# Gate and expert stage of a retrieval block in one block of instructions, coefficients two tiles behind, and one softmax

## The chip, the cores and the metric

The kernel runs on one core of a Trainium2 chip. The time is that of the device in microseconds (us), from the first to the last instruction of the core. The median of three runs is given; beside it stands one execution taken by the hardware profiler, from which every row comes. Five engines work side by side, each on its own list of instructions, and wait for one another by semaphores: TensorE (PE in the rows, its weight loads PEld), VectorE (DVE), ScalarE (ACT), GpSimd (POOL) and SyncE (SP). An engine's name with a q behind it is its instruction queue, where it issues transfers. Sixteen DMA engines move the data.

## What is computed

A decoder block on 512 tokens of width 1024: two token mixers in parallel (a short gated convolution and a gated delta rule), and then a retrieval of experts. The change lies in the retrieval, cut here to its core:

```python
q = (h @ w_q).reshape(B, T, HEADS, 2, 128)           # 8 heads, 2 halves
s = einsum('bthpd,hpnd->bthpn', q, sub_keys)          # 128 keys per half
v1, i1 = top_k(s[..., 0, :], 16); v2, i2 = top_k(s[..., 1, :], 16)
top_s, pos = top_k(v1[..., :, None] + v2[..., None, :], 16)
eidx = take(i1 * 128 + i2, pos)                       # 16 of 16384 experts per head
gates = softmax(top_s)
act = gelu(einsum('btd,bted->bte', h, u_tab[eidx]))
out = einsum('bte,bted->btd', gates * act, v_tab[eidx])
x = x + gt2 * rmsnorm(out, norm_post_ffn)
```

## The kernel before

The 512 tokens are four tiles of 128. Three of them (384 tokens) are computed densely: the products with all 16384 rows of u_tab are made in 128 tiles of 128 experts ("U tiles"), GELU is applied, the result is multiplied with a dense matrix of gates that is zero almost everywhere (the coefficient), and the product with the rows of v_tab ("V tiles") is summed in six PSUM banks. The fourth tile (the "fetched" or own tokens) is treated sparsely: GpSimd fetches one expert row per token at a time (line 201), 128 rows of u_tab and 128 of v_tab, and VectorE multiplies and sums them. Four row buffers are used in turn, so a fetch waits until the row four before it is used.

All products are made in three parts, with every operand split in a high and a low part: ScalarE makes the high part of a weight tile (1024 elements in each partition), GpSimd or VectorE the low part, and a U tile is 24 matmuls, a V tile 18. Three stages follow one another, each an `nc.Block()`, at whose end all engines meet at a barrier.

**Retrieval** (retrieve_stage). TensorE makes the 16 query pieces, then 68 U tiles (`early`). For the fetched tokens the top-k of eight heads runs first on VectorE (`topk(VA, ...)`), then `shift(VO, ...)`, the list of rows `own_row` (line 1653) and a softmax of their own (lines 1631 to 1654). ScalarE makes its Exp at line 1511, in the order of its list between U piece 0 and U piece 1. Then follows the top-k of the dense tokens with `shift(VP, ...)` and `softmax(VP, ...)` at its end. GpSimd makes the low parts (line 1527); from the sixth U piece on its list has a fetch ahead of each of them.

**Gates** (scatter_stage). The dense gates are made by one-hot matrices: six rounds of eight units of 8 tokens. VectorE makes hot1 (line 1739) and the weighted hot2 (line 1744); for units 3 and 7 ScalarE makes hot2 (lines 1815 and 1821). TensorE multiplies them (line 1787), ScalarE copies the result to `gate_block` (line 1834), SP stores it in four quarters of 512 KB (line 1861). Beside this run six U tiles a round (line 1795), behind units 0, 1, 2, 4, 5 and 6. In the last round the last two of them stand behind unit 7. SP also issues the first two U tiles (line 1867) and four V tiles (line 1869) of the next stage, and at the end waits for all its stores (line 1895). The GELUs of the 104 U tiles made before the expert stage are stored in DRAM.

**Experts** (expert_stage). 24 of the U tiles remain, and all 128 V tiles. TensorE alternates: U tile p+1, then V tile p, and for the last 104 V tiles there is no U tile beside. For each tile p ScalarE makes GELU, the high parts of U tile p+2, of the coefficient (`split_c`) and of V tile p+1; VectorE the low part of U tile p+1, of V tile p, the coefficient (line 2117), its low part and one to three fetched rows (`own_rows_at`). SP loads U tiles, V tiles, the stored GELUs and, once for four tiles, the gates (lines 1948 and 1963). At the end the four token tiles are normalized and stored one by one.

## Time and profile before

| | us |
|---|---|
| median of 3 runs | 1856.44 (1854.17 to 1859.69) |
| span of the profiled execution | 1856.8 |
| TensorE busy | 1768.2 (95%) |
| VectorE busy | 1307.3 (70%) |
| GpSimd busy | 764.5 (41%) |
| ScalarE busy | 742.8 (40%) |
| matmuls of the V tiles, three groups | 294.6, 294.5, 294.1 |
| mean granted clock of TensorE | 0.981 |

The share of an engine is an average over stages that have different limits. TensorE's matmuls are pipelined: a duration of one reaches into the next, so starts are to be compared and not durations summed. The granted clock is given as a share of full speed (1.0 is 2.4 GHz, 0.5 is 1.2 GHz).

### The profile page before, as it was taken

How to read it: one execution, taken by the hardware profiler on the slowest of the kernel's cores; microseconds unless marked ns; L12 is line 12 of the kernel's file. 1: busy time of each engine (PE TensorE's matmuls, PEld its weight loads, DVE VectorE, ACT ScalarE, POOL GpSimd, SP SyncE). 2: the span in 40 equal slices, each digit the busy share in tenths (PEclk: the TensorE clock that was granted, in tenths of full speed). 3: DMA queues.
4: the chain of work that ended last, by engine and by line, in shares of the span. 5: the costliest groups of instructions: out<-in, count | busy, mean ns of one | idle time of the engine just before them, and what ended most of it. 6: DMA issues, size and time to landing. Idle time of an engine off the chain costs nothing. (4 is left out here: it accounts for less than half of the span.)

```text
span 1856.8 us, 31058 instructions
## 1 busy us (share of the span) xinstructions
PE 1768.2 (95%) x11485; PEld 1564.7 (84%) x11485; DVE 1307.3 (70%) x2777; ACT 742.8 (40%) x1227; POOL 764.5 (41%) x449
## 2 busy tenths in 40 slices
PE   3999999999998989999999999879999999999998
PEld 2666888878877889999999999879998888888887
DVE  5993454553224679878869999756787888777777
ACT  4332332242234233333337767633333333333334
POOL 2333232344442448777753333122454443332330
PEclk9998999999999999999999999989999999999999
DMA  9661101022322249888868999978899999889883
GB/s 356 217 233 71 36 16 34 25 91 91 102 79 103 91 141 314 282 292 292 286 235 281 341 311 331 319 264 285 287 317 337 370 370 359 326 320 328 316 325 145
DMA packets 179267, 432.64 MB, mean 233 GB/s; under 512 B 15816, under 2 KB 91720, under 8 KB 179040
## 3 DMA queue, kind: packets, MB, share of 16 engines
q1 hardware_dynamic: 125088, 273.71, 42.5%
q0 software_dynamic: 36864, 134.23, 20.3%
q10 hardware_dynamic: 17216, 23.36, 3.4%
q8 instruction: 63, 1.03, 0.2%
q14 instruction: 36, 0.29, 0.0%
HBM read 383.54 MB, written 47.71 MB: 232 GB/s over the span
## 5 line engine op out<-in xcount | busy, mean ns | idle before, releaser
L201 POOL DMA_INDIRECT own_rows<-in_peer_v_dram,own_row x128 | 212.3, 1659 | 330.8 <-DVE y_own L2094 312.7
L1988 PE MATMUL banks<-v_hi,coef_lo 128*128 128x512 f32 x756 | 294.6, 390 | 0.0
L1988 PE MATMUL banks<-v_lo,coef_hi 128*128 128x512 f32 x756 | 294.5, 390 | 0.0
L1988 PE MATMUL banks<-v_hi,coef_hi 128*128 128x512 f32 x756 | 294.1, 389 | 0.1
L201 POOL DMA_INDIRECT own_rows<-in_u_rows_dram,own_row x128 | 160.6, 1255 | 233.1 <-DVE own_rows L1733 178.8
L2079 DVE TENSOR_TENSOR v_lo<-weight_ring,v_hi 128x1024 fp32r<-128x1024 f32 x128 | 156.5, 1222 | 24.7 <-ACT v_hi L2027 22.7
L1988 PEld LDWEIGHTS banks<-v_hi,coef_hi 128*128 128x128 f32 x756 | 142.0, 188 | 29.5 <-issue 0.5
L1988 PEld LDWEIGHTS banks<-v_hi,coef_lo 128*128 128x128 f32 x756 | 141.9, 188 | 29.5
L1988 PEld LDWEIGHTS banks<-v_lo,coef_hi 128*128 128x128 f32 x756 | 141.9, 188 | 28.9
L2094 DVE SCALAR_TENSOR_TENSOR y_own<-own_rows,own_coef,y_own 128x1024 f32<-128x1024 f32 x128 | 163.8, 1279 | 1.9 <-DVE y_own L2094 0.5
L1397 PE MATMUL banks<-h_hi,wring_hi 128*128 128x384 f32 (+2 forms) x448 | 155.2, 347 | 4.0 <-ACT gelu_early L1479 2.9
L2027 ACT ACTIVATE v_hi<-weight_ring 128x1024 fp32r<-128x1024 f32 x128 | 135.1, 1055 | 59.4 <-PE banks L1988 48.1
L1527 POOL TENSOR_TENSOR wring_lo<-weight_ring,wring_hi 128x1024 fp32r<-128x1024 f32 x54 | 129.6, 2399 | 65.4 <-ACT wring_hi L1469 65.3
L1397 PE MATMUL banks<-h_lo,wring_hi 128*128 128x384 f32 (+2 forms) x448 | 154.0, 344 | 0.0
L1397 PE MATMUL banks<-h_hi,wring_lo 128*128 128x384 f32 (+2 forms) x448 | 153.9, 344 | 0.0
L2031 ACT ACTIVATE coef_hi<-coef 128x384 fp32r<-128x384 f32 x128 | 67.0, 524 | 211.6 <-DVE coef L2117 211.6
L1469 ACT ACTIVATE wring_hi<-weight_ring 128x1024 fp32r<-128x1024 f32 x54 | 57.3, 1061 | 158.4 <-PE banks L1397 157.9
L1665 DVE SCALAR_TENSOR_TENSOR own_rows<-own_rows,banks 128x1024 f32<-128x1024 f32 x64 | 77.8, 1215 | 52.3 <-DMA own_rows<-in_u_rows_dram,own_row 52.3
L2079 DVE TENSOR_TENSOR coef_lo<-coef,coef_hi 128x384 fp32r<-128x384 f32 x128 | 71.3, 557 | 57.5 <-ACT coef_hi L2031 57.5
L2117 DVE TENSOR_TENSOR coef<-gelu,gate_tiles 128x384 f32<-128x384 f32 x128 | 70.8, 553 | 45.8 <-ACT gelu L2041 45.8
L1165 POOL TENSOR_TENSOR wring_lo<-weight_ring,wring_hi 128x1024 fp32r<-128x1024 f32 x26 | 64.1, 2465 | 88.7 <-ACT wring_hi L1185 88.7
L1787 PE MATMUL banks<-query_hot 128*128 128x128 f32 x768 | 93.6, 278 | 6.7 <-ACT gate_block L1834 5.0
(393 smaller groups left out, 4346.1 us busy)
## 6 DMA issues: line engine op xcount, KB each, us to landing
weight_ring<-in_peer_v_dram SPq DMA_DIRECT2D x128, 512.0 KB, 5.4
weight_ring<-in_peer_u_dram SPq DMA_DIRECT2D x68, 512.0 KB, 4.5
ada<-in_w_ada_dram SPq DMA_DIRECT2D x48, 512.0 KB, 5.7
gate_scratch<-gate_block SPq DMA_DIRECT2D x48, 512.0 KB, 7.0
gate_tiles<-gate_scratch SPq DMA_DIRECT2D x32, 768.0 KB, 6.9
gelu_scratch<-gelu_early ACTq DMA_DIRECT2D x104, 192.0 KB
gelu<-gelu_scratch SPq DMA_DIRECT2D x104, 192.0 KB, 5.6
u_early<-in_peer_u_dram SPq DMA_DIRECT2D x36, 512.0 KB, 7.1
```

The lines of the kernel that those rows point to most:

```text
L201: pool.indirect_dma_start(own_rows[:, n % R], None, tables[n // NS], bass.IndirectOffsetOnAxis(ap=own_row[:, n % NS:n % NS + 1], axis=0)). ...
L1165: nc.gpsimd.tensor_tensor(w_lo[:, b % 2], wring[:, b], w_hi[:, b % 2].bitcast(F32), ALU.subtract).then_inc(lo_ready, 1)
L1397: last = nc.tensor.matmul(out, ww[n % HR][:, k, :], x[:, k, t0:nt], start=(k == 0 and m == 0), stop=(k == KT - 1 and m == 2))
L1527: nc.gpsimd.tensor_tensor(w_lo[n % HR][:], w[:, n % WR], w_hi[n % HR][:].bitcast(F32), ALU.subtract).then_inc(lo_ready, 1)
L1665: nc.vector.scalar_tensor_tensor(rows[:, i % R], rows[:, i % R], 1.0, h_psum[:], ALU.mult, ALU.mult, accum_out=own_act[:, bass.ds(n, 1)]). ...
L1787: last = nc.tensor.matmul(bank[2 * (u % 2) + t // 4][:, t % 4 * P:(t % 4 + 1) * P], hot1[:, u % RH, t, :], hot2[:, u % RH, t, :], start=Tr ...
L1988: last = nc.tensor.matmul(y_bank(t, half)[:], w[:, j, t * P:(t + 1) * P], x[:, j, c], start=(first and n == 0), stop=False)
L2027: nc.scalar.activation(v_hi[:, e % G], vt[:, e % G], ACT.Copy).then_inc(v_hi_ready, 1)
L2031: nc.scalar.activation(c_hi[:, e % G], coef[:, e % 2], ACT.Copy).then_inc(c_hi_ready, 1)
L2079: return nc.vector.tensor_tensor(dst, src, hi.bitcast(F32), ALU.subtract)
L2094: nc.vector.scalar_tensor_tensor(y_own[:], rows[:, n % R], own_coef[:, n - NS:n - NS + 1], y_own[:], ALU.mult, ALU.add).then_inc(row_used, 1)
L2117: nc.vector.tensor_tensor(by_block(coef[:, p % 2]), by_block(gel[:, j]), gt[:, i % 2, :, j, :], ALU.mult).then_inc(coef_ready, 1)
```

## The change

Three edits. First, the barrier between gates and experts goes: both stages are written into one `nc.Block()`, the semaphores of both are made ahead of it (`scatter_sems`), and TensorE waits for the copy of unit 6 instead. SP issues U tiles 2 and 3 of the expert stage behind the last stores and only then waits for the stores; the wait for the stored GELUs moves from ScalarE to SP. In the last round the U tiles stand where they do in the other rounds, and unit 7 gets its hot2 from VectorE. Tiles in SBUF are laid out in another order, and `y_own` is zeroed behind the wait for the first gate tile. Second, LAG = 2: in the expert stage the coefficient and everything behind it are made two tiles later; TensorE runs U tile m and then V tile m-3. Third, in the retrieval the softmax of the fetched tokens is no longer made ahead of the dense top-k; one softmax over all four token tiles is made at the end.

```diff
                 retrieve_stage(nc, a, env, acts)
-                scatter_stage(nc, a, env, spill, acts)
-            expert_stage(nc, a, env, spill, acts, out)
+                scatter_sems(env)
+                block = late.enter_context(nc.Block())
+                scatter_stage(nc, a, env, spill, acts, block)
+            expert_stage(nc, a, env, spill, acts, out, block)
...
                     if m == 0:
                         copy(0)
-                        act.wait_ge(*VO.after("gsub"))
-                        nc.scalar.activation(gates[:, ND], gates[:, ND], ACT.Exp).then_inc(own_exp, 1)
...
                 act.wait_ge(*VP.after("gsub"))
-                nc.scalar.activation(gates[:, 0:ND], gates[:, 0:ND], ACT.Exp).then_inc(exped, 1)
+                nc.scalar.activation(gates[:], gates[:], ACT.Exp).then_inc(exped, 1)
...
                 dve.wait_ge(*VA.after("sel1", PH - 1))
-                shift(VO, ND, TT)
...
-                softmax(VO, ND, TT, own_gate[:].rearrange("p (h k) -> p h k", h=PH), "own_gate")
...
-                shift(VP, 0, ND)
-                softmax(VP, 0, ND, th(gates[:, 0:ND]), "gates")
+                total, top = (gsum[:, n].rearrange("p t h -> p (t h)") for n in range(2))
+                nc.vector.tensor_copy(top, th(score)[:, :, 0]).then_inc(*VP.step("gmax"))
+                dve.wait_ge(*VP.after("gmax"))
+                nc.vector.tensor_tensor(th(gates), th(score), top.unsqueeze(2).to_broadcast([P, TT * PH, TOPK]), ALU.subtract).then_inc(*VP.step("gsub"))
...
+                nc.vector.tensor_tensor(own_gate[:].rearrange("p (h k) -> p h k", h=PH), gates[:, ND], top[:, ND * PH:TT * PH].unsqueeze(2).to_broadcast([P, PH, TOPK]),
+                                        ALU.mult).then_inc(*VP.step("own_gate"))
...
-        tiles = {False: {u: (m,) for m, u in enumerate(U_UNITS)},
-                 True: {**{u: (m,) for m, u in enumerate(U_UNITS[:-2])}, NU - 1: (U_ITER - 2, U_ITER - 1)}}
+        tiles = {u: (m,) for m, u in enumerate(U_UNITS)}
...
+        def act_makes(u, final):
+            return u in by_act and not (final and u == NU - 1)
...
+            body(NR - 1, True)
+            pe.wait_ge(*A.after(f"unit{NU - 2}", NR - 1))
...
+            for q in range(1, NQ):
+                store(NR * SLOTS - 1, 1, q)
+            for m in range(2, 4):
+                sp.wait_ge(u_lo_ready, m - 1)
+                sp.dma_start(ut[:, m % 2], a["peer_u"][N_EARLY + m]).then_inc(s_u[m % 2], 16)
+            for s in stored:
+                sp.wait_ge(s, 16 * NQ * (NR + 1))
+            for s in s_gel:
+                sp.wait_ge(s, G0 + 16 * (NR * U_ITER // 2))
...
+        LAG = 2
...
+            for j in range(G):
+                u_products(j, j % 2)
+                if j > LAG:
+                    y_products(j - LAG - 1, j - LAG - 1, first=(j == LAG + 1))
+            with pe.Fori(1, GL) as i:
+                for j in range(G):
+                    u_products(i * G + j, j % 2)
+                    y_products(i * G + (j - LAG - 1), (j - LAG - 1) % G)
+            with pe.Fori(GL, GX) as i:
+                for j in range(G):
+                    y_products(i * G + (j - LAG - 1), (j - LAG - 1) % G)
...
+            for m in range(NX + LAG):
+                p = m - LAG
...
+                if m < NL:
+                    act.wait_ge(u_done, m + 1)
+                    nc.scalar.activation(gel[:, m % G, :], bank[m % 2][:, 0:TD], ACT.Gelu).then_inc(gelu_ready, 1)
+                if m + 2 < NL:
+                    split_u(m + 2)
+                if p >= 0:
                     split_c(p)
                     if p + 1 < NX:
                         split_v(p + 1)
...
+            n = U_DONE
+            for m in range(NX + LAG):
+                p = m - LAG
+                if m + 1 < NL:
+                    split_u(m + 1)
+                if p < 0:
+                    continue
...
+                if p == 0:
+                    nc.vector.memset(y_own[:], 0.0).then_inc(own_zero, 1)
```

## Rows read from the trace of the kernel before

**Rows 1.** Windows: us, busy us (instructions) of each engine, PEclk, DMA share, GB/s

```profile
683.30:689.40 6.10, 6.09 (x19) 6.09 (x20) 1.97 (x14) 1.43 (x2) 4.53 (x5) 0.50 0.79 253
1202.00:1206.00 4.00, 4.00 (x21) 4.00 (x21) 0.00 (x0) 1.08 (x2) 0.00 (x0) 0.65 0.07 20
1206.80:1215.00 8.20, 6.34 (x37) 6.02 (x35) 3.99 (x6) 2.04 (x3) 1.35 (x1) 1.00 0.95 292
1225.00:1228.00 3.00, 3.00 (x10) 3.00 (x11) 1.94 (x2) 1.94 (x2) 0.00 (x0) 0.50 0.70 171
1500.00:1600.00 100.00, 100.00 (x443) 82.84 (x442) 82.28 (x99) 37.89 (x51) 38.57 (x23) 1.00 0.96 357
```

**Rows 2.** Waits of TensorE from 560 us on: us in total, times, longest

```profile
PE banks L1978 <- PEq L1726: 11.8, 1, 11.8
PE banks L1787 <- ACT gate_block L1834: 5.0, 1, 5.0
PE banks L1397 <- POOL wring_lo L1527: 0.7, 1, 0.7
```

**Rows 3.** The chain that ended last, from 1224.95 us: start, us, work

```profile
1224.95 10.31 PE banks L1978 x48
...
1239.39 4.18 PE banks L1978 x24
...
1426.29 416.44 PE banks L1988 x1836
```

**Rows 4.** Timeline of TensorE at the gates' end: start, us, instruction, wait before

```profile
1192.16 3.73 PE L1787 MATMUL banks<-query_hot 128*128 128x128 f32 x32
1200.88 3.78 PE L1787 MATMUL banks<-query_hot 128*128 128x128 f32 x16 [4.98 <-ACT gate_block L1834]
```

**Rows 5.** Timeline of ScalarE in the same stretch

```profile
1194.20 2.45 ACT L1815 ACTIVATE query_hot<-cst,idxT 128x128 f32<-128x128 f32 x8 [0.40 <-PE banks L1787]
...
1199.77 2.01 ACT L1834 ACTIVATE gate_block<-banks 128x512 f32<-128x512 f32 x4
1204.70 1.08 ACT L1834 ACTIVATE gate_block<-banks 128x512 f32<-128x512 f32 x2 [2.91 <-PE banks L1787]
```

**Rows 6.** Timeline of VectorE in the same stretch

```profile
1188.81 2.15 DVE L1744 TENSOR_SCALAR query_hot<-cst,idxT,gateT 128x128 f32<-128x128 f32 x8
1190.86 1.23 DVE L1739 TENSOR_TENSOR query_hot<-cst,idxT 128x1024 f32<-128x1024 f32 x1
...
1211.01 1.23 DVE L1758 TENSOR_TENSOR wring_lo<-u_tile,wring_hi 128x1024 fp32r<-128x1024 f32 x1 [16.33 <-ACT wring_hi L1847]
```

**Rows 7.** Line 1867, U tiles 0 and 1, issued at 1176.5 and 1180.7

```profile
DMA to landing us min/median/max: 9.6/10.8/12.0
```

**Rows 8.** Timeline of all engines at the start of the U pieces

```profile
680.20 0.31 ACT L1511 ACTIVATE gates<-gates 128x128 f32<-128x128 f32 x1 [3.99 <-DVE gates L1646]
...
680.40 0.23 DVE L1653 CAST own_row<-own_row_f 128x128 uint32<-128x128 f32 x1
...
683.31 0.69 PE L1397 MATMUL banks<-h_hi,wring_hi 128*128 128x384 f32 x1 [2.94 <-ACT gelu_early L1479]
...
684.04 1.14 POOL L201 DMA_INDIRECT own_rows<-in_u_rows_dram,own_row  x1 [0.16 <-issue]
...
690.38 1.22 DVE L1665 SCALAR_TENSOR_TENSOR own_rows<-own_rows,banks 128x1024 f32<-128x1024 f32 x1 [4.97 <-DMA own_rows<-in_u_rows_dram,own_row]
...
692.85 2.40 POOL L1527 TENSOR_TENSOR wring_lo<-weight_ring,wring_hi 128x1024 fp32r<-128x1024 f32 x1
```

**Rows 9.** Timeline of VectorE among the V tiles

```profile
1434.44 1.22 DVE L2079 TENSOR_TENSOR v_lo<-weight_ring,v_hi 128x1024 fp32r<-128x1024 f32 x1
1435.58 0.55 DVE L2117 TENSOR_TENSOR coef<-gelu,gate_tiles 128x384 f32<-128x384 f32 x1
1436.05 1.28 DVE L2094 SCALAR_TENSOR_TENSOR y_own<-own_rows,own_coef,y_own 128x1024 f32<-128x1024 f32 x1
1437.24 0.55 DVE L2079 TENSOR_TENSOR coef_lo<-coef,coef_hi 128x384 fp32r<-128x384 f32 x1
```

## What I expect of the change, and why

> **What bounds the kernel now.** I read the windows first, then the waits of TensorE, then the chain of waits, and last the timelines of single engines around each wait. In the expert stage TensorE is busy 100.00 of 100 us at a granted clock of 1.00, and the DMA engines are near their limit beside it (share 0.96, 357 GB/s) [rows 1]. The chain of waits says the same: from 1426.29 us one piece of 1836 matmuls runs for 416.44 us, which is 102 tiles of 4.08 us, and a product with a U tile takes 4.18 us for 24 matmuls [rows 3]. So from 1224.95 us to the end nothing but matmuls counts, and a gain has to come from places where TensorE stands still. From the retrieval on the change touches four: 11.8 us at the block boundary (PEq L1726), 5.0 us for a copy of the gates (gate_block), 2.9 us for a GELU at the start of the retrieval, 0.7 us for a wring_lo behind it [rows 2, 8]. Each idle stretch of 2.9 us or more also drags a slow one behind it: after the 2.94 us the granted clock was 0.50 for 6.1 us, which is 1.2 of 2.4 GHz, and at the start of the expert stage again 0.50 [rows 1]. There 48 matmuls took 10.31 us [rows 3], where two U tiles at full clock take 2 x 4.18 = 8.36: 1.95 us lost. After the 5 us wait 16 matmuls took 3.78 us where 32 took 3.73 before it [rows 4]: 1.9 us again.
>
> **The boundary between gates and experts.** Reference point: TensorE finishes unit 4 and U tile 3 of the last round, then units 5 and 6 start at 1192.16, and U tile 1 of the expert stage ends at 1224.95 + 10.31 = 1235.26 [rows 3, 4]. In between lie 3 units (3.73 / 2 = 1.87 with the pipeline's end, 1.75 from start to start) and 4 U tiles of 4.18: 5.25 + 16.7 = 22.0 us of work in 43.1 us. So 21.1 us are lost here, of which 16.8 are the two waits and about 4 are clock.
>
> The change moves three things. (1) Unit 7 of the last round gets its weighted one-hot from VectorE instead of ScalarE. On ScalarE it is the eight L1815 from 1194.20 and the L1821 up to the next copy at 1199.77, 5.6 us in front of the copies of units 5 and 6 [rows 5]; that is what TensorE waited 5.0 us for. On VectorE it costs 8 selections in 2.15 us behind the 1.23 us comparison that it makes already [rows 6]; VectorE stood idle for 16.33 us up to 1211.01, so this is hidden. Before that idle time it split tile 5, ready at 1194.7, and that can't come earlier; unit 7 is then ready at 1194.7 + 3.3 = 1198.0. (2) The last two U tiles go behind units 5 and 6. TensorE then runs unit 5 from 1192.16, tile 4, unit 6, tile 5, unit 7 without a wait and ends at 1192.16 + 5.25 + 8.36 = 1205.8; unit 7 is asked for at 1204.0, long after 1198.0. (3) The barrier goes; U tile 0 of the expert stage follows at once (its split is done by 1202) and ends at 1209.95.
>
> What is late next is on ScalarE and on SP's queue. ScalarE copies unit 7 at 1205.9 to 1207.0 (1.08 us [rows 5]), makes a v_hi and the hi part of U tile 1 (about 1.05 each), VectorE the lo part: 1210.3, a wait of 0.4 us, so TensorE ends U tile 1 at 1214.5. U tile 2 is the trouble. SP issues it behind the four stores of the last gate block, and these wait for the copy of unit 7, now 1207.0 where it was 1205.8. Before, the engines were busy with these stores from 1206.8 to 1215.0 at a share of 0.95 and 292 GB/s, two GELU stores included [rows 1]. Shifted, the stores hold the engines from 1208.0 to 1216; U tile 2 (512 KB, 1.5 us at the 357 GB/s of [rows 1]) is queued behind them, and up to three fetched rows that now fall in the same time take their share. I take a landing at 1218.5; hi, lo and hand-over take 2.5 us, so U tile 2 starts at 1221.0. The bounds: 1219.0 if the rows are all through before the stores, and 1224.9 if it lands 12.0 us after an issue at 1210.4, as the slower of the two first U tiles did in a full queue [rows 7]; I stay near the lower end because the engines were all but empty from 1202 to 1206 (share 0.07 [rows 1]), where now the first rows go. Then TensorE was idle 6.5 us and restarts at the lower clock; I charge 1.95 us as before. Gain of the boundary: 1235.26 - 1221.0 - 1.95 = **12.3 us** (8.4 to 14.3).
>
> The Trainium skill, page "DMA: Bandwidth & Descriptors", section "Queues, rings and completion order", says that on each engine the descriptors of one queue are consumed in ring order. By that rule U tile 2 can't pass the stores, which is the case that I take; the 9.6 to 12.0 us of the two loads issued into a busy queue [rows 7] agree with it.
>
> What SP issues behind: the first gate tile now waits for the last store (about 1216.5) and is queued behind U tiles 2 and 3. It would land near 1224, at worst 12 us after its issue, 1228.5. The coefficient of tile 0 is two tiles later than before: V tile 0 is multiplied only after U tile 3, at about 1231. VectorE stands at this load with the lo part of U tile 4 queued behind it, needed at 1235. Both are met; cost nothing, and if the load came after 1229.5 each us would count. U tile 4 is behind two gate tiles of 768 KB; it lands near 1226 and is needed after 1227. The zeroing of y_own (0.9 us) moves behind the gate wait on VectorE, in the same cover.
>
> **From U tiles to V tiles alone.** The coefficient of tile p is now finished by ScalarE after the GELU of tile p+2. While U and V products alternate (8.3 us a pair) this leaves slack on both sides. When the U tiles end, ScalarE makes coef_hi of tile 21 only after the GELU of tile 23, and tiles 21, 22 and 23 have three fetched rows each on VectorE. One such tile costs 1.14 (v_lo) + 0.47 (coef) + 0.47 (coef_lo) + 3 x 1.19 = 5.65 us, from start to start [rows 9], against 4.08 us of TensorE. With the end of U tile 23 as zero, coef_lo of 21 is ready at 1.5, of 22 at 7.1, of 23 at 12.8 and of 24 at 18.0; TensorE asks for them at 4.1, 8.2, 12.3 and 17.0. That is 0.6 + 1.0 = **1.6 us lost** (0 if VectorE is further ahead, 4 if a row lands late).
>
> **The retrieval's softmax.** Before, ScalarE stopped at the Exp of the fetched tokens (started 680.20) and split the next weight piece only afterwards; VectorE had its list of rows at 680.40, and GpSimd could fetch only at 684.04 behind the split that came late; TensorE stood from 680.37 to 683.31 [rows 8]. Removed are one Exp with its two table loads on ScalarE and five small VectorE operations. Now ScalarE splits at 676.2, when U piece 1 ends, GpSimd needs 2.4 us [rows 8], and the fetch starts with the list, at 680.4: 3.6 us earlier. But the next GpSimd split (692.85) stands behind a fetch that waits for the first row used, and the row takes 6.3 us (684.04 to 690.38) [rows 8]. So this split ends at 691.6 instead of 695.25. TensorE has its work up to 680.37 + 2 x 4.18 = 688.7 and waits 2.9 us there, in place of 2.94 us before the slow stretch and 0.7 after it. The next start is 3.6 us earlier. Whether the clock falls again costs 0 to 3.1 us (6.1 us at half clock were the 3.1); I take 1.7, since the wait is about as long as the one that did it. Gain **1.9 us** (0.5 to 3.6), and TensorE is the bound for the rest of the retrieval, so it lasts. At the end the joint softmax is 512 instead of 384 elements wide for shift, Exp and sum, and one product is added: about 0.5 us on VectorE, most of it beside U tiles and transposes. I charge 0.1 us (0 to 0.5).
>
> **Sum.** -12.3 - 1.9 + 0.1 + 1.6 = -12.5 us on the profiled 1856.8 us, 1844.3. The median of the runs is 0.4 us lower, so **1844.0 us**.
>
> **Rivals.** (a) The load lands late: rows and stores share the engines and U tile 2 lands up to 12 us after its issue. Then it starts at 1224.9, the boundary gives 8.4 and the whole 8.6: 1847.8. For it speaks the store rate of 292 GB/s at a share of 0.95, against it that only 1.5 MB of rows are in the way. (b) U tile 2 is not held by the stores and lands while U tile 1 runs. Then there is neither wait nor slow clock: the boundary gives 1235.3 - 1214.5 = 20.8 and the time is 1835.4. It needs the load to overtake 2 MB that were issued before it. (c) The backlog of fetched rows at the end of the U tiles is not worked off at once, because rows are fetched one by one behind VectorE: 6 instead of 1.6 us, 1848.4. (d) The stall is moved and not removed: the stage of V tiles alone starts with empty buffers and gives back what the boundary gained, 1853 to 1856. Against it, the time per tile there was that of TensorE. (e) Slower: DMA becomes the bound of the V tiles alone. There 35.7 MB move in 100 us, 24.5 tiles, 1.46 MB a tile; at 357 GB/s this is 4.08 us, exactly TensorE's tile. If loads and rows bunch differently, so that only 340 GB/s come through, a tile takes 4.28 us, and 104 tiles cost 21 us: 1865. It decides from 4.20 us a tile, 347 GB/s; the share of 0.96 leaves little room, but what is moved and when it is asked for stays the same.
>
> **Chances.** Forecast (U tile 2 starts by 1223, 1841 to 1846.5) 0.55; (a) 0.19; (b) 0.08; (c) 0.08; (d) 0.06; (e) 0.04. The likeliest case gives 1844.0. The range reaches from the early end of the boundary (1842 less 3.6 for the retrieval and the U end without loss) to beyond (a) and (c): 1838.5 to 1850.0. A measurement of this kernel tells about 0.3%, 5.6 us, from no change. Faster: 0.55 + 0.19 + 0.08 + 0.08, less 0.02 for (a) and (c) together, 0.88; same: (d) and that 0.02, 0.08; slower: (e), 0.04.
>
> **What would show it.** Right: no 5.0 us and no 11.8 us wait of TensorE; unit 7 followed at once by a product of the expert stage; then one wait of 5 to 8 us before U tile 2, released by the lo part of that tile, with its load landing 8 to 9 us after its issue; in the retrieval a wait of about 3 us before the sixth U piece, released by GpSimd, and none for the GELU; two short waits of about 1 us each when the U tiles end, released by coef_lo; V tiles of 4.08 us. Wrong: a wait for gate_tiles on VectorE that reaches TensorE, a V tile above 4.1 us over a long stretch, or the first U tile of the expert stage waiting for its split.

## The result, and the profile of the changed kernel

| | before | changed kernel |
|---|---|---|
| median of 20 runs, us | 1858.59 | 1860.37 |
| lowest to highest, us | 1854.17 to 1864.41 | 1857.77 to 1866.41 |
| profiled span, us | 1856.8 | 1857.5 |

The ratio is 1.0016 with a 95% interval of 1.0008 to 1.0023. The forecast was 12.5 us less; the median rose by 1.8 us, far below the 2% from which a change counts as one. The waits that were to go are gone all the same. These are TensorE's waits from 560 us on in the changed kernel (line waited at, what ended the wait: us in total, times, longest), to be laid beside [rows 2]:

```profile
PE banks L1990 <- DVE wring_lo L2093: 8.9, 2, 8.8
...
PE banks L1399 <- POOL wring_lo L1527: 2.3, 1, 2.3
PE banks L2000 <- DVE coef_lo L2093: 2.0, 2, 1.1
```

The 11.8 us and the 5.0 us have gone. One wait of 8.8 us before U tile 2 has come, and two of about 1 us for coef_lo at the end of the U tiles. Now the chain of waits from the last gate unit on (start, us, work), which answers to [rows 3]:

```profile
1198.80 1.80 PE banks L1793 x16
...
1200.62 1.09 ACT gate_block L1841 x2
...
1202.79 5.59 SPq L1866
...
1208.42 1.45 SPq L1866
...
1209.91 5.82 DMA u_tile<-in_peer_u_dram
...
1218.13 9.91 PE banks L1990 x48
1228.04 4.20 PE banks L2000 x18
1232.24 4.18 PE banks L1990 x24
...
1414.71 428.64 PE banks L2000 x1836
```

Two readings. TensorE began U tile 2 at 1218.13 us and two U tiles were done at 1228.04, where before it was 1235.26: TensorE is 7.2 us ahead there, with two U tiles of 4.18 us more behind it, 15.6 us in all. And in the last line 1836 matmuls take 428.64 us where they took 416.44 [rows 3]. They begin 11.6 us earlier (1414.71 against 1426.29) and last 12.2 us longer. That is the whole difference of the two profiles. Three windows of the changed kernel (us, busy us and instructions of each engine, granted clock, DMA share, GB/s) say what it isn't:

```profile
682.00:686.00 4.00, 4.00 (x25) 4.00 (x24) 2.19 (x10) 1.44 (x2) 1.88 (x2) 1.00 0.91 316
...
1214.00:1218.00 4.00, 0.00 (x0) 0.00 (x0) 1.15 (x1) 2.24 (x3) 0.00 (x0) 0.52 1.00 361
...
1500.00:1600.00 100.00, 100.00 (x430) 80.60 (x429) 78.72 (x94) 37.20 (x49) 38.10 (x21) 1.00 0.88 332
```

In the first, behind the old place of the 2.9 us wait, TensorE works at full clock, where it had 0.50 before [rows 1]. In the second it stands and waits for U tile 2 while the DMA engines are busy throughout. In the last one TensorE is busy for all 100 us at a granted clock of 1.00, as in [rows 1], but gets through 430 matmuls instead of 443. It waits for nothing, the clock is full, and the DMA engines have become less busy (0.88 for 0.96): each matmul takes longer. The timeline of TensorE shows the step (start, us, instruction):

```profile
1499.72 0.39 PE L2000 MATMUL banks<-v_lo,coef_hi 128*128 128x512 f32 x1
1499.95 0.40 PE L2000 MATMUL banks<-v_hi,coef_lo 128*128 128x512 f32 x1
1500.18 0.39 PE L2000 MATMUL banks<-v_hi,coef_hi 128*128 128x512 f32 x1
1500.42 0.40 PE L2000 MATMUL banks<-v_lo,coef_hi 128*128 128x512 f32 x1
1500.65 0.39 PE L2000 MATMUL banks<-v_hi,coef_lo 128*128 128x512 f32 x1
1500.88 0.40 PE L2000 MATMUL banks<-v_hi,coef_hi 128*128 128x512 f32 x1
```

From start to start it is (1500.88 - 1499.72) / 5 = 232 ns; over the whole stretch 428.64 / 1836 = 233.5 ns, before 416.44 / 1836 = 226.8. In these 102 tiles the 6.7 ns a matmul make 12.2 us. A V tile that stands between two U tiles takes 4.20 us in the chain above, and before it was this:

```profile
1243.57 4.12 PE banks L1988 x18
```

That is 0.08 us a tile or 1.9 us for the 24 of them, so that the slower V matmuls cost about 14 us altogether. The U tiles kept their 4.18 us.

The change does one thing that the section on it names in half a sentence, that its diff leaves out and that the prediction gave no price. It lays out the SBUF tiles of the expert stage in another order:

```diff
-        gel = sb(ctx, "gelu", [P, G, TD])
...
         v_hi = sb(ctx, "v_hi", [P, G, D], F32R)
         v_lo = sb(ctx, "v_lo", [P, G, D], F32R)
-        gt = sb(ctx, "gate_tiles", [P, 2, TD // TB, G, TB])
+        own_coef = sb(ctx, "own_coef", [P, NS])
+        ss = sb(ctx, "y_sq", [P, 4, TT])
         coef = sb(ctx, "coef", [P, 2, TD])
+        gel = sb(ctx, "gelu", [P, G, TD])
         c_hi = sb(ctx, "coef_hi", [P, G, TD], F32R)
         c_lo = sb(ctx, "coef_lo", [P, G, TD], F32R)
-        own_coef = sb(ctx, "own_coef", [P, NS])
...
+        gt = sb(ctx, "gate_tiles", [P, 2, TD // TB, G, TB])
...
-        ss = sb(ctx, "y_sq", [P, 4, TT])
```

Tiles are put one behind another, and y_sq has 64 bytes a partition (4 x 4 fp32). Before it was the last of them. Now it stands ahead of coef_hi and coef_lo, and moves them by 64 bytes against v_hi and v_lo: coef_hi begins at byte 191008 of a partition before and at 179296 now, v_hi at 142880 and 136736. Modulo 256 these are 32 for both before, and 96 against 32 now. Every other tile that lies or lay between the two is a multiple of 256 bytes long, and so is the distance from v_hi to v_lo and from coef_hi to coef_lo.

### The profile page after: what moved, and what is told of

It is laid out like the page before. It is cut to its first block and busy times, and to the rows that moved or that the text cites. A ratio compares the mean times of both kernels' runs of the same rounds, so it can differ in the third digit from the quotient of the medians.

```text
span 1857.5 us, 31015 instructions
## 1 busy us (share of the span) xinstructions
PE 1775.6 (96%) x11485; PEld 1558.8 (84%) x11485; DVE 1311.6 (71%) x2781; ACT 736.1 (40%) x1208; POOL 768.6 (41%) x449
## 5 line engine op out<-in xcount | busy, mean ns | idle before, releaser
L201 POOL DMA_INDIRECT own_rows<-in_peer_v_dram,own_row x128 | 217.1, 1696 | 332.9 <-DVE y_own L2108 315.5
L2000 PE MATMUL banks<-v_hi,coef_hi 128*128 128x512 f32 x756 | 298.9, 395 | 2.0 <-DVE coef_lo L2093 2.0
L2000 PE MATMUL banks<-v_hi,coef_lo 128*128 128x512 f32 x756 | 298.8, 395 | 0.0
L2000 PE MATMUL banks<-v_lo,coef_hi 128*128 128x512 f32 x756 | 298.8, 395 | 0.0
L1801 PE MATMUL banks<-h_hi,wring_hi 128*128 128x384 f32 x288 | 99.2, 345 | 0.0
L1527 POOL TENSOR_TENSOR piece_lo<-weight_ring,piece_hi 128x1024 fp32r<-128x1024 f32 x28 | 67.1, 2397 | 72.4 <-ACT piece_hi L1471 72.3
```

The source lines that it names most:

```text
L201: pool.indirect_dma_start(own_rows[:, n % R], None, tables[n // NS], bass.IndirectOffsetOnAxis(ap=own_row[:, n % NS:n % NS + 1], axis=0)). ...
L1527: nc.gpsimd.tensor_tensor(w_lo[n % HR][:], w[:, n % WR], w_hi[n % HR][:].bitcast(F32), ALU.subtract).then_inc(lo_ready, 1)
L1801: last = nc.tensor.matmul(bank[4 + m % 2][:, 0:TD], ww[:, m % 2, k, :], x[:, k, 0:TD], start=(k == 0 and n == 0), stop=(k == KT - 1 and n ...
L2000: last = nc.tensor.matmul(y_bank(t, half)[:], w[:, j, t * P:(t + 1) * P], x[:, j, c], start=(first and n == 0), stop=False)
```

## The experiments

In all of them the time is set beside runs of the kernel before on the same chip.

**Is it the layout? (e1, e2).** e1 is the changed kernel with y_sq allocated last again, and nothing else; e2 is the kernel before with 64 bytes put ahead of coef.

```diff
e1:
-        ss = sb(ctx, "y_sq", [P, 4, TT])
         coef = sb(ctx, "coef", [P, 2, TD])
...
         y = sb(ctx, "y", [P, TT, D])
+        ss = sb(ctx, "y_sq", [P, 4, TT])
e2:
+        sb(ctx, "pad", [P, 16])
         coef = sb(ctx, "coef", [P, 2, TD])
```

> The changed kernel with one edit: y_sq, 64 bytes in each partition, is laid out behind y as before the change and no longer between own_coef and coef, so coef, gelu, coef_hi and coef_lo start 64 bytes lower, at 32 modulo 128 as in the kernel before. Theory P (the place of coef_hi and coef_lo in SBUF sets the pitch of the V matmuls): the pitch falls from 233.3 back to 226.7 ns, a V tile from 4.20 to 4.08 us, 128 tiles give 15 us, about 1845 us beside 1858.6 of the kernel before. Rival C (the pitch comes from the new instruction order of TensorE, its loops or the lag of two tiles): pitch and time stay, 233.3 ns and 1860 us. Rival D (from the load on SBUF by the DMA queues and VectorE, which the new order shifts): likewise unchanged.

> The kernel before with one edit: an unused tile of 64 bytes in each partition ahead of coef, so coef, coef_hi and coef_lo start 64 bytes higher, at 96 modulo 128. Theory P: the pitch of the V matmuls rises from 226.7 to 233.3 ns, 128 tiles cost 15 us, about 1874 us. Rivals C and D: 226.7 ns and 1858.6 us, since order and load are those of before.

e1 took 1848.37 us, 0.9950 (0.9932 to 0.9968) of before; e2 took 1871.85 us, 1.0086 (1.0060 to 1.0112). The chain of e1, then that of e2 (whose piece holds 1872 matmuls):

```profile
1415.46 416.40 PE banks L2000 x1836
```

```profile
1417.15 436.90 PE banks L1989 x1872
```

The first is 226.8 ns a matmul, the second 233.4. The same 64 bytes make a fast kernel slow and a slow one fast, with all instructions the same. The theory that the layout is the cause holds, and the queues, the lag and the merged block have no part in the slow matmuls.

**Which placement is good? (e3, e4).** e3 is e1 with 96 bytes behind eps, so that all large tiles begin at a multiple of 128 bytes; e4 is e1 with y_sq between coef_hi and coef_lo, so that only coef_lo is moved.

```diff
e3:
         eps = sb(top, "eps", [P, 1])
+        sb(top, "pad", [P, 24])
e4:
         c_hi = sb(ctx, "coef_hi", [P, G, TD], F32R)
+        ss = sb(ctx, "y_sq", [P, 4, TT])
         c_lo = sb(ctx, "coef_lo", [P, G, TD], F32R)
```

> As the kernel with y_sq last, and 96 unused bytes behind eps, so nearly all large tiles start at 0 modulo 128 instead of 32. If the cost under theory P is one of 128-byte lines that an operand crosses, the fixed 13.3 ns that a 512-column matmul takes beyond 512 columns at 2.4 GHz shrinks in all stages: 7 ns for some 10000 matmuls would be 60 us or more, about 1780 us. If only the step from 32 to 96 matters, pitches stay at 226.7 and 173.3 ns and the time at about 1845 us.

> The changed kernel with y_sq between coef_hi and coef_lo: coef_hi starts at 32 and coef_lo at 96 modulo 128. Theory P with a cost for each matmul whose stationary operand lies at 96: one in three V matmuls uses coef_lo, so the mean pitch is 226.7 + 6.7 / 3 = 228.9 ns, a V tile 4.12 us, and the time about 1850 us. If the cost hangs on coef_hi alone, 226.7 ns and 1845 us; if on any of coef or gelu, which VectorE and ScalarE use, 226.7 ns too.

e3 took 1847.07 us (416.41 us for the 1836): aligning everything gives no more than e1 had. e4 took 1855.74 us, and the groups of instructions by shape show it between 1410 and 1830 us (busy us, mean ns of one; in e1 all three stand at 389):

```profile
L2000 PE MATMUL banks<-v_hi,coef_lo 128*128 128x512 f32 x605 | 240.3, 397 | 0.0
L2000 PE MATMUL banks<-v_lo,coef_hi 128*128 128x512 f32 x605 | 237.2, 392 | 0.0
L2000 PE MATMUL banks<-v_hi,coef_hi 128*128 128x512 f32 x605 | 235.4, 389 | 0.9 <-DVE coef_lo L2093 0.9
```

By these durations the matmul with the moved operand is longer, that before it a little, the third not. A duration reaches into the next matmul, though. From start to start (547 or 548 of each kind between 1440 and 1820 us) the matmul with coef_lo takes 235.9 ns, v_lo with coef_hi 229.2 and v_hi with coef_hi 228.3, where all three take 226.4 to 227.0 in e1. So the one whose operands lie apart loses 9 ns and its two neighbours about 2 each. The 1836 took 424.55 us, 231.2 ns each: two thirds of the loss, where only one matmul in three uses coef_lo. The forecast of a third was wrong, and why the neighbours lose too stays open.

**One operand's place, or the two against each other? (e5, e6, e9, e10).** Each is e1 with pads: 64 bytes ahead of v_hi, behind v_lo and behind coef_lo (e5); 32 bytes ahead of coef_hi (e6); 64 bytes ahead of v_hi alone, which moves v and the coefficients together (e9); 64 bytes ahead of gate_tiles, which leaves all four operands in place (e10). In one diff, with the experiment behind each line (the pads' names differ from file to file):

```diff
+        sb(ctx, "pad_a", [P, 16])   # e5, e9
         v_hi = sb(ctx, "v_hi", [P, G, D], F32R)
         v_lo = sb(ctx, "v_lo", [P, G, D], F32R)
+        sb(ctx, "pad_b", [P, 16])   # e5; [P, 32] in e13, [P, 64] in e14
         own_coef = sb(ctx, "own_coef", [P, NS])
...
+        sb(ctx, "pad", [P, 8])      # e6
         c_hi = sb(ctx, "coef_hi", [P, G, TD], F32R)
         c_lo = sb(ctx, "coef_lo", [P, G, TD], F32R)
+        sb(ctx, "pad_c", [P, 16])   # e5, e10
         gt = sb(ctx, "gate_tiles", [P, 2, TD // TB, G, TB])
```

> The kernel with the sums laid last (1848.4 us), plus three pads of 64 bytes: v_hi and v_lo now begin at 96 of 128 bytes, the coefficients stay at 32, and gate_tiles, y_own and y are at 96 as they are in the changed kernel. Theory 'it is the place of the stationary operand': the V products keep 226.7 ns a matmul (1836 matmuls in 416.4 us) and the time stays within 3 us of 1848.4. Rival 'any fp32 tile of the V products, or the tiles that VectorE and the DMA use beside them, counts': 233.3 ns, 428.5 us, about 1861.

> The kernel with the sums laid last, with a pad of 32 bytes ahead of coef_hi, so that coef_hi and coef_lo begin at 64 of 128 bytes. So far 0 and 32 gave 226.7 ns and 96 gave 233.3. Theory A, a row of 32 bytes more at 96 straddles something that 0 to 64 don't: 226.7 ns, about 1848. Theory B, the half above 64 is the slow one: 233.3 ns, about 1861.

> The kernel with the sums laid last, with one pad of 64 bytes ahead of v_hi: v_hi, v_lo, coef_hi and coef_lo all begin at 96 of 128 bytes, the gate tiles, y_own and y too. So far the V products took 226.7 ns a matmul with both operands at 32 or both at 0, and 233.3 with the operands at different remainders (32 and 96, 96 and 32, 32 and 64). Theory D, only the difference of the two operands' places counts: 226.7 ns, 416.4 us for the 1836, about 1848.4. Theory A, an operand that begins at 64 or above of 128 bytes costs, whichever it is: 233.3 ns, about 1861.

> The kernel with the sums laid last, with one pad of 64 bytes ahead of gate_tiles: all four operands of the V products stay at 32 of 128 bytes, gate_tiles, y_own, y and the sums go to 96. In every slow kernel so far these had moved too. Theories D and A (the operands count): 226.7 ns, about 1848.4. Rival G, it is what VectorE, ScalarE and the DMAs touch beside the matmuls: 233.3 ns, about 1861.

| kernel | v_hi, coef_hi, modulo 256 | difference | 1836 matmuls, us | median, us |
|---|---|---|---|---|
| e1 | 32, 32 | 0 | 416.40 | 1848.37 |
| e3 | 128, 128 | 0 | 416.41 | 1847.07 |
| e9 | 96, 96 | 0 | 416.41 | 1847.19 |
| e10 | 32, 32 | 0 | 416.41 | 1849.40 |
| e14 | 32, 32 | 0 | 416.45 | 1846.57 |
| e6 | 32, 64 | 32 | 428.64 | 1860.81 |
| changed | 32, 96 | 64 | 428.64 | 1860.37 |
| e5 | 96, 160 | 64 | 428.64 | 1859.28 |
| e13 | 32, 160 | 128 | 426.88 | 1858.26 |

Here are the pieces of 1836 matmuls of e6 and then of e9:

```profile
1413.90 428.64 PE banks L2001 x1836
```

```profile
1416.54 416.41 PE banks L2001 x1836
```

My first theory blamed the place of the stationary operand (the coefficients; v is the moving one), and it is e9 that refutes it: with coef_hi and coef_lo at 96 the matmuls are fast if v is at 96 as well, and in the changed kernel, with v at 32, they are slow. e5 does not do so by itself. I counted modulo 128 when I wrote down what I expected of it, and modulo 256 its pads moved the coefficients too, from 32 to 160. e6 came out at the 233 ns of its theory B, that the half above 64 is the slow one, and e9 refutes this as well. e10 clears gate_tiles, y_own, y and y_sq; own_coef, coef and gelu, the other tiles of this stage that the pads shift, are in their old place in the slow e6 and moved in the fast e9. What is left is the difference between the two operands of a product.

**Modulo what? (e13, e14).** e1 with 128 and with 256 bytes ahead of own_coef.

> The kernel with the sums laid last, with a pad of 128 bytes ahead of own_coef: the coefficients begin 128 bytes off the places of v_hi and v_lo, modulo 512. Theory, the difference counts modulo 128 (or a smaller power of two above 32): 226.7 ns, 1848.4 us. Rival, it counts modulo 256 or 512: 233.3 ns, about 1861 us.

> The same with a pad of 256 bytes. Modulo 128 or 256: 226.7 ns, 1848.4 us. Modulo 512: 233.3 ns, about 1861 us.

Their pieces, e13 first:

```profile
1415.59 426.88 PE banks L2001 x1836
```

```profile
1410.17 416.45 PE banks L2001 x1836
```

128 bytes apart is slow (1858.26 us, a shade less: 232.5 ns), 256 apart is fast (1846.57 us). So it counts modulo 256; of the two answers I had thought the other likelier. e13's coefficients were at 128-byte alignment with v_hi, so aligning to 128 bytes would not have been enough. In all slow kernels the coefficients lie 32, 64 or 128 bytes further on than v; other differences were not run.

**Does it hold for other products? (e11).** e1 with 64 bytes between h_hi, h_lo and the weight rings. All that follows moves along, so v and the coefficients still agree, both at 96.

```diff
+        sb(top, "pad", [P, 16])
         ring = sb(top, "weight_ring", [P, WRING, D])
```

> The kernel with the sums laid last, with one pad of 64 bytes between h_hi/h_lo (which stay at 32 of 128 bytes) and the weight rings: the split weights and all that follows go to 96, so that the U products have their operands 64 apart and the V products theirs at the same remainder. Theory D: V products at 226.7 ns (416.4 us for 1836), U products slower, 180.0 instead of 173.3 ns for 384 columns if the same 6.67 ns are added; 24 x 128 of these alone cost 20.5 us and the projections more: 1870 to 1890. Theory A: V products at 233.3 (both at 96), U products slow too: 1883 to 1903. If neither slows: 1848.

It took 1866.34 us, 18.0 more than e1. The V products stayed fast (416.43 us), the U products, with 384 columns, became slower; these are pieces of its chain of waits:

```profile
1405.13 4.24 PE banks L1991 x24
1409.37 4.08 PE banks L2001 x18
1413.45 4.25 PE banks L1991 x24
1437.00 416.43 PE banks L2001 x1836
```

In the retrieval and the gates, over some 2200 matmuls of 384 columns, it is 176.6 ns from start to start for the 173.4 of e1. The direction is as expected, the size is about half of it (3.2 ns where 6.67 were added), and the time lies below the 1870 to 1890 us that were forecast: with 384 columns the loss is smaller than with 512. In the expert stage it hardly shows, since the U tile takes 4.24 for 4.18 us and the V tile beside it 4.08 for 4.12. Most of it comes earlier. The products of 512 columns with the same weights ahead of the retrieval take 233.2 ns for 227 to 228, and the first U piece starts at 677.51 us instead of 664.85.

**The retrieval's term (e7).** e1 with the old, separate softmax of the fetched tokens: the retrieval's hunks of the diff ahead are undone, nothing else.

> The kernel with the sums laid last, but with the softmax of the fetched tokens done by itself at the list of rows, as in the kernel before; everything behind the retrieval is the changed kernel's. My reading of the traces is that the merged softmax gives 4.4 us in the retrieval (forecast: 1.9): so 1848.4 + 4.4 = 1852.8 us, with a wait of 2.9 us for a GELU, a granted clock of 0.50 behind it, and the gate stage starting about 4.4 us later. Rival: the gain belongs to a drift that the projection stage has anyway; then 1849.5 or less.

Its profile has the wait of 2.9 us for the GELU back, the granted clock from 680 to 700 us is 0.83 (0.91 in e1), and the span is 1850.5 us against 1846.0. But its five times are 1852.31, 1848.00, 1852.68, 1848.48 and 1849.03. The median, 1849.03, is 0.7 above e1's and within the rival's "1849.5 or less", and the ratio to before is 0.9950 as in e1: with five runs and four the times don't tell the two apart.

The profiles say more. Of the 4.5 us between the two spans, 1.7 were there before the retrieval's first U piece (666.50 against 664.85 us), where both kernels run the same code. So I measure from the start of this piece to the first matmul of the gates. With the softmax apart this takes 303.5 to 303.7 us (before, e2, e7). With one softmax there are two groups: 299.0 to 299.4 us in the six kernels whose granted clock from 680 to 700 us is 1.00 (the changed kernel, e4, e12, e14, e15, e17), and 300.9 to 302.0 in the nine where it is 0.91 (e1, e3, e5, e6, e8, e9, e10, e13, e16). The edit is worth about 4.4 us if the clock stays up behind the remaining wait for GpSimd, and about 2.3 if it falls.

**The load behind the stores (e8, e12, e15).** In e8 SP issues U tile 2 ahead of the copy of unit 7 and of the last four stores, U tile 3 behind the first.

```diff
e8:
+                    if not more and u == NU - 1:
+                        expert_u(2)
...
+            expert_u(3)
             for q in range(1, NQ):
                 store(NR * SLOTS - 1, 1, q)
-            for m in range(2, 4):
-                sp.wait_ge(u_lo_ready, m - 1)
-                sp.dma_start(ut[:, m % 2], a["peer_u"][N_EARLY + m]).then_inc(s_u[m % 2], 16)
```

> The kernel with the sums laid last, but SP issues U tile 2 of the expert stage ahead of the copy of unit 7 and of the last four stores, and U tile 3 behind the first of these stores. Theory, the 8.5 us wait of TensorE is the load standing behind the issue of the stores: the wait falls below 1 us, no slow clock behind it, and the U tile starts 8 us earlier; the gate tiles still come behind the stores, so a wait of up to 3 us for the first coefficient may take its place. 1848.4 - 8 - 1.5 to - 6: 1839 to 1842.5 us. Rival, the time is given back further on (gate tiles land late, TensorE waits 8 us before V tile 0): 1847 to 1849.

1845.35 us, 3.0 less than e1, where 6 to 9 had been expected. The ratio to before, 0.9942 (0.9924 to 0.9960), is not to be told from e1's 0.9950 (0.9932 to 0.9968). TensorE's waits from 1180 us on before and behind this edit, e1 and then e8:

```profile
PE banks L1990 <- DVE wring_lo L2093: 8.6, 2, 8.5
PE banks L2000 <- DVE coef_lo L2093: 2.6, 2, 1.6
```

```profile
PE banks L2004 <- DVE coef_lo L2097: 10.1, 3, 7.4
...
PE banks L1994 <- DVE wring_lo L2097: 0.2, 1, 0.2
```

The wait for the U tile has gone and one of 7.4 us for the first coefficient has come. VectorE's timeline names its cause, the gate tile, which SP could issue only at 1214.91 us, when the last store had landed:

```profile
1219.30 0.91 DVE L2134 MEMSET y_own<- 128x1024 f32 x1 [5.67 <-DMA gate_tiles<-gate_scratch]
```

e12 therefore stores first the quarter of the last block that holds the first expert tiles, loads the gate tile behind it, and stores the other three quarters after that. The second gate tile and the zeroing of y_own, now one tile later, wait for these.

```diff
e12, SP:
-                        store(i * SLOTS + 1, 1, 0)
+                        store(i * SLOTS + 1, 1, 0 if more else NQ - 1, None if more else g_["last_store"])
...
-            for q in range(1, NQ):
-                store(NR * SLOTS - 1, 1, q)
-            for s in stored:
-                sp.wait_ge(s, 16 * NQ * (NR + 1))
+            sp.wait_ge(g_["last_store"], 16)
...
             sp.dma_start(gt[:, 0], spill[:, tile_at(0) // G]).then_inc(s_g[0], 16)
+            g_["blocks_left"]()
...
                 if j == G - 1 and i < GX - 1:
+                    if not i:
+                        sp.wait_ge(*g_["blocks_out"])
```

> The kernel e8 (U tiles 2 and 3 issued ahead of the last stores), and of the last gate block the quarter that holds the first expert tiles is stored first, with a semaphore of its own; the first gate tile is loaded behind it and the other three quarters are stored after that; y_own is zeroed one tile later. In e8 TensorE waited 7.4 us for the first coef_lo because the gate tile was issued at 1214.9 us and landed at 1219.3. Theory: it is now issued at about 1207 and lands by 1213, the wait for coef_lo falls below 1 us, and the time is 1845.4 - 7 = 1838 us (1836.5 to 1840). Rival, the next load (V or U tile behind the three stores) takes the wait over: 1843 to 1846.

It was slower, 1850.64 us (ten runs, 1846.78 to 1857.10), 5.3 more than e8 and above both what was expected and the rival. The profile is that of the fastest of the ten. The gate tile was used at 1213.26 us, but SP then stood at the wait for the last stores ahead of the second gate tile, with U tile 4 queued behind it:

```profile
1208.77 4.54 SPq L1866 DMA_DIRECT2D gate_scratch<-gate_block  x3
1218.76 0.35 SPq L1983 DMA_DIRECT2D gate_tiles<-gate_scratch  x1
1219.15 0.63 SPq L1971 DMA_DIRECT2D u_tile<-in_peer_u_dram  x1
```

ScalarE waited for that tile 11.94 us and had the coefficient queued behind it; TensorE waited 10.5. e15 puts the last two stores behind U tile 4 and the second gate tile behind U tile 5, and y_own is zeroed at tile 5.

```diff
e15, SP:
+                if p == 4:
+                    g_["blocks_left"](1)
+                    g_["blocks_left"](2)
+                if p == 5:
+                    sp.wait_ge(*g_["blocks_out"])
+                    sp.dma_start(gt[:, 1], spill[:, tile_at(G) // G]).then_inc(s_g[1], 16)
```

> The kernel e12, with the last two stored quarters issued behind U tile 4 and the second gate tile behind U tile 5, so that no load that is due soon stands behind a wait of SP. In e12 the gate tile had landed at 1213.3 us, but ScalarE stood at the hi part of U tile 4, issued at 1219.2, with the coefficient queued behind it, 10.5 us of TensorE. Theory: U tile 4 is issued at 1212 and lands by 1219; the wait for coef_lo falls to 0 to 1 us: 1850.6 - 10 - 2 for the clock: 1836 to 1841 us. Rival, loads, stores and rows share the engines, and whatever is issued first only moves the wait to the next: 1845 or more.

1838.71 us, 0.9897 (0.9880 to 0.9913) of before, in the middle of what was expected, and clear of e1 and e8. The wait at this place is 2.3 us.

**The lag (e16, e17).** e16 is e1, and e17 is e15, with one line changed:

```diff
-        LAG = 2
+        LAG = 1
```

> The kernel with the sums laid last, coefficients one tile behind instead of two. V tile 0 is then due behind U tile 2 and the gate tile is not there yet (VectorE had it at 1221 in the kernel after), and V products wait for the GELU chain within a pair of tiles. Theory: the wait for U tile 2 stays near 8.5, V tile 0 is due at about 1222.5 and waits 2 to 4 us, and the 2.6 us at the end of the U tiles changes to between 0 and 4: 1849 to 1853 us. Rival, the gate tile comes in time because TensorE is late anyway: 1847 to 1848.5.

> The kernel e15 with a lag of one tile. In e15 the first coef_lo came at 1219.1 us although the gate tile had landed at about 1213, because ScalarE makes coef_hi of tile 0 behind the hi part of U tile 4. With the lag of one it stands behind U tile 3, which lands about 1210. Theory: no wait of more than 1 us for coef_lo at the start, and that at the U tiles' end falls from 2.6 us to 0.6 as in e16: 1838.7 - 2.3 - 2.0 = 1834.5 us (1832 to 1837). Rival, V tile 0, due a tile earlier, waits for the gate tile instead: 1837 to 1840.

e16 took 1843.36 us, 5.0 less than e1, where I had expected it to be slower. TensorE's waits from 1180 us on:

```profile
PE banks L1990 <- DVE wring_lo L2093: 9.0, 2, 8.8
PE banks L2000 <- DVE coef_lo L2093: 0.6, 1, 0.6
```

The 2.6 us at the end of the U tiles have become 0.6. V tile 0 did not wait for the gate tile at all: by the chain it follows U tile 2 at once, at 1223.56 us. The other 3 us no wait accounts for. The two kernels ran on different chips, and the runs of the kernel before beside e16 have a median 1.9 us lower (1857.04 against 1858.91); the ratios to before, 0.9928 (0.9911 to 0.9944) and 0.9950 (0.9932 to 0.9968), overlap. In the profiles e16 is 2.9 us ahead when the retrieval's first U piece starts (661.94 against 664.85), where the code is the same. So only the 2.0 us are shown. e17 took 1837.73 us, 0.9891 (0.9871 to 0.9910) of before, the lowest median of all and 22.6 us under the changed kernel, but not to be told from e15. The forecast of 1832 to 1837 failed and the rival's came: its first coefficient still made TensorE wait 2.4 us, for the gate tile this time.

## Why the prediction was wrong

- **The step that failed** is a term that isn't in the sum: "Against it, the time per tile there was that of TensorE", said of rival (d), and the 4.08 us a tile that the whole account of the last 416 us rests on. A matmul's duration was taken as given by its shape. It depends on where its operands lie as well: about 14 us, 1.9 in the pairs of U and V tiles and 12.2 in the V tiles alone. Rival (e) had the symptom, a V tile of 4.20 us, and the wrong cause: it made the DMA the bound, and its share had fallen to 0.88. The last paragraph of the prediction named "a V tile above 4.1 us over a long stretch" as what would refute it, and that is where the trace was to be read first.
- **Without that** the forecast is near. e1, the change with the old remainders, has a median 10.5 us below that of before on its chip; 12.5 were forecast, and its 1848.4 us lies in the range. Some of it is luck: in its profile 1.4 us were there ahead of the retrieval. The terms by themselves give 10.0 for the boundary and 2.2 for the retrieval, less 2.6 at the end of the U tiles, which is 9.6 us.
- **The boundary**, 12.3 us forecast. In the changed kernel unit 5 started at 1186.74 us (1192.16 before), U tile 2 at 1218.13: 31.4 us later, where 28.8 were forecast. Of the 15.6 us by which TensorE is ahead, 5.4 were there at unit 5, so the boundary gave 10.2. The term was 2.5 us too large at the load and 0.4 too small at the clock, for which 1.95 us had been charged (9.91 - 8.36 = 1.55 us lost; in e1 10.40 - 8.36 = 2.04). Units 5, 6 and 7 and the two U tiles ran on with a single wait of 0.16 us, as worked out.
- **The load** was late for another reason than the one given. I had it issued early and waiting in the queue behind the stores for 8 to 9 us; it was issued only at 1209.91 us, because SP spent 8.1 us on issuing the four stores, and landed 5.82 us later. With the 5.4 us by which this kernel is ahead at unit 5 added, that is an issue at 1215.3, where 1210.4 was taken, and a landing at 1221.2, where 1218.5 was. The Trainium skill, page "DMA: Bandwidth & Descriptors", section "Queues, rings and completion order", has a queue's descriptors consumed in order on each DMA engine, and adds that they need not complete in order, so the prediction's "can't pass the stores" is more than it says. The rows agree with the order: the last store had landed by 1214.71 us, when SP could issue the gate tile, and U tile 2 landed behind it at 1215.74. But the order bit at the issue already.
- **The retrieval**, 1.9 us forecast (0.5 to 3.6): 4.4 in the changed kernel's profile (the gates begin 5.4 us earlier, of which 1.0 was there before the retrieval), since the clock didn't fall after the 2.33 us wait at 689.97; 2.2 in that of e1, where it fell after 2.97 us. The wait itself is as forecast (2.3 for 2.9 us, released by GpSimd). The sum took one middle value, 1.7 us, for a clock that either falls or doesn't; my reading of the result, on which e7's forecast of 4.4 us rested, took one profile for a constant.
- **The end of the U tiles**: 1.6 us forecast, 2.0 in the changed kernel, 2.6 in e1, released by coef_lo. Right in kind, somewhat small. That a lag of one would have had most of the gain without this loss (0.6 us in e16) was not seen.

## What to carry to other kernels

When a change moves tiles in SBUF, write down the start of both operands of the matmuls that bound the kernel, modulo 256, before and after; a 64-byte tile put in between cost this kernel as much as the whole restructuring gave (12 us between the changed kernel and e1, beside 10.5 between e1 and before). In a stretch where TensorE never waits, count matmuls per 100 us at a clock of 1.00 first: if the count falls, it isn't a wait. And a load that is due soon must stand ahead of the stores, and of every wait for them, on its issuing queue, or the stall is only handed on (8.8, 7.4, 10.5 and then 2.3 us here).

## What the runs showed of the hardware

- Back-to-back fp32r matmuls of 512 columns take 226.8 ns when the stationary and the moving operand start at the same byte modulo 256, and 233.5 when they start 32 or 64 bytes apart (232.5 at 128 apart). The absolute place made no difference (32, 96 and 128 were all fast). With 384 columns it was 176.6 for 173.4 ns at 64 apart (e11 and e1). If only the stationary operand of every third matmul lies apart, that one takes 235.9 ns and the two others 228.3 and 229.2 (e4). Why it is so no run here shows.
- The Trainium skill, page "SBUF — State Buffer", section "SBUF: two separate sides", has TensorE never waiting for anyone among the engines. No run here tests it: e10 moved the others' tiles without effect, but none took their accesses away. What the runs show is that the duration of a matmul hangs on the places of its own two operands together.
- An idle TensorE doesn't always fall to the lower of its two clocks on restart, and the length of the idle time alone didn't decide it here. At one place of the retrieval, over fifteen kernels, the granted clock from 680 to 700 us stayed at 1.00 after waits of 2.19 to 2.59 us and was 0.91 after waits of 2.49 to 3.64 us (2.59 in e4, without a fall, and 2.49 in e6, with one). It cost about 2 us.
- Issuing a transfer can itself take long: SP needed 8.1 us to issue the four stores of 512 KB in the changed kernel (0.40 to 5.59 us for a single one), and the load behind them on its list went out only then, at 1209.91 us.
